# An attention layer's steps reordered on every engine, with one weight split moved to GpSimd

## What is computed

```python
def swa_sink_attention(h, w_qkv, q_gain, k_gain, sinks, w_o):
    qkv = h @ w_qkv                      # [256, 1024] @ [1024, 1536]
    ...
    q = rmsnorm(q, q_gain)               # 16 query heads of 64
    k = rmsnorm(k, k_gain)               # 4 key heads
    ...
    scores = jnp.einsum('bnqkgd,bnskd->bnkgqs', qb, kw).astype(jnp.float32) * scale
    ...
    scores = scores + alibi[None, None]
    scores = jnp.where(mask[None, :, None, None], scores, -jnp.inf)
    ...
    logits = jnp.concatenate([scores, sink_col], axis=-1)
    p = jax.nn.softmax(logits, axis=-1)[..., :-1]
    out = jnp.einsum('bnkgqs,bnskd->bnqkgd', p.astype(vw.dtype), vw)
    ...
    return out @ w_o                     # [256, 1024] @ [1024, 1024]
```

## Time and profile before

| | |
|---|---|
| Median of 3 runs | 1288.05 us (1287.56 to 1288.16) |
| Profiled execution | 1287.21 us, span 1285.4 us |
| PE busy | 1254.6 us (98%) |
| DVE busy | 894.6 us (70%) |
| ACT busy | 711.4 us (55%) |
| POOL busy | 155.2 us (12%) |
| Mean DMA rate | 175 GB/s |

### The profile page before, as it was taken

How to read it: one execution, slowest core, us unless ns; L and a number is a source line. 1 busy time by engine, 2 the same in 40 slices (tenths; PEclk the granted TensorE clock), 3 DMA queues, 4 the chain that set the end, 5 groups by cost and what they waited for, 6 DMA issues and landing times.

```text
span 1285.4 us, 19450 instructions
## 1 busy us (share of the span) xinstructions
PE 1254.6 (98%) x7940; PEld 1121.1 (87%) x7940; DVE 894.6 (70%) x1148; ACT 711.4 (55%) x909; POOL 155.2 (12%) x171
## 2 busy tenths in 40 slices
PE   8999999999799999999999999999999999999997
PEld 7889888889689888889888888889999989988886
DVE  6866656566866755568777665678899886866666
ACT  5445554455665555444764444447997873544442
POOL 0000000005604000010010000020325432100000
PEclk9999999999899999999999999999999999999999
DMA  8676665645059666666147555545544435555551
GB/s 281 201 227 178 209 196 179 200 152 191 34 147 213 204 191 196 197 164 215 66 135 255 199 185 184 187 144 161 157 153 122 153 99 193 201 196 196 196 190 41
DMA packets 214888, 224.52 MB, mean 175 GB/s; under 512 B 7312, under 2 KB 192016, under 8 KB 214672
## 3 DMA queue, kind: packets, MB, share of 16 engines
q1 hardware_dynamic: 211472, 213.41, 52.1%
q10 hardware_dynamic: 2304, 7.77, 1.8%
q0 software_dynamic: 1024, 2.10, 1.0%
HBM read 222.20 MB, written 1.05 MB: 174 GB/s over the span
## 4 chain that ended last, share of the span: by engine, by line
PE 84%; DVE 9%; ACT 3%; issue 2%; POOL 1%; DMA 1%; SPq 0%; DVEq 0%; ACTq 0%
PE ps L521 21%; PE ps L748 18%; PE ps L512 12%; PE ps L532 7%; PE ps L542 5%; PE ps L710 5%; PE ps L1040 3%; PE ps L504 3%; DVE wlo L1653 2%; PE ps L493 2%; PE ps L495 2%; PE ps L494 2%; DVE ssm_taps L2107 1%; ACT whi L1155 1%; PE ps L1021 1%
## 5 line engine op out<-in xcount | busy, mean ns | idle before, releaser
L1653 DVE TENSOR_TENSOR wlo<-raw,whi 128x2048 fp32r<-128x2048 f32 x199 | 456.5, 2300 | 127.0 <-ACT whi L1155 126.4
L1155 ACT ACTIVATE whi<-raw 128x2048 fp32r<-128x2048 f32 x202 | 385.3, 1910 | 87.9 <-PE ps L748 29.8
L521 PE MATMUL ps<-act,whi 128*128 128x512 f32 x1200 | 285.3, 390 | 0.4 <-DVE sum_sb L1796 0.4
L521 PEld LDWEIGHTS ps<-act,whi 128*128 128x128 f32 x1200 | 223.2, 188 | 45.7 <-DVE sum_sb L1796 0.7
L512 PEld LDWEIGHTS ps<-act,wlo 128*128 128x128 f32 x1416 | 180.8, 191 | 6.8 <-DVE wlo L1653 1.0
L512 PE MATMUL ps<-act,wlo 128*128 128x256 f32 x1416 | 183.9, 283 | 0.5 <-DVE wlo L1653 0.5
L1212 ACT ACTIVATE low_sb<-ps 128x512 f32<-128x512 f32 x88 | 52.4, 596 | 200.0 <-PE ps L512 199.9
L532 PE MATMUL ps<-whi,act 128*128 128x256 f32 x736 | 133.1, 285 | 1.1 <-DVE act L1734 1.1
L532 PEld LDWEIGHTS ps<-whi,act 128*128 128x128 f32 x736 | 113.5, 192 | 2.7 <-DVE act L1734 1.3
L1796 DVE TENSOR_TENSOR sum_sb<-ps,low_sb 128x512 f32<-128x512 f32 x88 | 60.5, 688 | 76.4 <-ACT low_sb L1212 76.3
L748 PE MATMUL ps<-whi,hidhi 128*128 128x512 f32 x336 | 104.2, 391 | 0.2 <-DVE sum_sb L1796 0.2
(11 more groups left out here) (238 smaller groups left out, 1848.4 us busy)
## 6 DMA issues: line engine op xcount, KB each, us to landing
raw<-in_mlp_w SPq DMA_DIRECT2D x128, 512.0 KB, 4.5
raw<-in_ffn_w_gate_up SPq DMA_DIRECT2D x88, 512.0 KB, 5.2
raw<-in_ssm_w_in SPq DMA_DIRECT2D x50, 512.0 KB, 4.8
raw<-in_ffn_w_down SPq DMA_DIRECT2D x44, 512.0 KB, 4.9
raw<-in_conv_w_in SPq DMA_DIRECT2D x24, 512.0 KB, 4.9
raw<-in_attn_w_in SPq DMA_DIRECT2D x18, 512.0 KB, 4.9
raw<-in_ssm_w_out SPq DMA_DIRECT2D x16, 512.0 KB, 4.5
raw<-in_attn_w_qkv SPq DMA_DIRECT2D x12, 512.0 KB, 4.4
```

The costliest lines, as they stand in the source:

```text
L521: e.matmul(bank2(b + f), hi[:, k, f * P:(f + 1) * P], act[:, :, k, :], start=k == 0, stop=False, skip_group_check=True)
L1155: e.activation(whi[s][:, :], raw[s][:, :], ACT.Copy).then_inc(*rounded.up(c))
L1653: e.tensor_tensor(wlo[s][:, :], raw[s][:, :], f32(whi[s][:, :]), ALU.subtract).then_inc(*split_by_vector.up(c))
```

## The change

Groups now alternate between token tiles, so that the first groups need only the first heads; the value block is projected third; attention steps are spread over blocks 3 to 5 and over the output products, on PE as below. Scores have one region (banks 2 and 3), odd groups mix in bank 5, and the output tiles gather in banks 0, 1, 7 and 2. The output weight comes in the order lower and upper columns of its first half, then of its second. On GpSimd the head rates and biases are interleaved anew, and behind the last bias it does the `lo` of block SWA + 8, which VectorE no longer does. The small per-head tiles are now six of each kind. Leaving `swa` aside, the other stages are the same.

```diff
+            return (split_by_pool if c in POOL_SPLITS.values() or c == SWA + 8 else split_by_vector)(c)
...
-            m, g = divmod(n, 4)
+            m, g = n % 2, n // 2
...
-        QKV_COLS = {"swa": (D, 0, 256, 512, 768, D + 256), "na": tuple(range(0, QKV2, WIDE))}
-        QKV_BANKS = {"swa": tuple((SWA + n) % SLOTS for n in range(5)) + (6,),
+        QKV_COLS = {"swa": (D, 0, D + 256, 256, 512, 768), "na": tuple(range(0, QKV2, WIDE))}
+        QKV_BANKS = {"swa": (1, 2, 0, 1, 0, 1),
                      "na": tuple((NA + n) % SLOTS for n in range(7)) + (6, 7)}
 
-        SCORES_AFTER = {"swa": (3, 4), "na": (5, 6)}
-
-        def score_bank(n):
-
-            return 2 * (n % 2) if n < 6 else 2
+        HEADS_OF = {"k0": 0, "k1": 0, "q0": 1, "q1": 3, "q2": 4, "q3": 5}
+        TURN_HEADS_IN = {"k0": 4, "q0": 5, "k1": 7, "q1": 7, "q2": 7, "q3": 7}
+        OUT_BANKS = {(0, 0): 0, (1, 0): 1, (0, 1): 7, (1, 1): 2}
+        SCORES_AFTER = (5, 6)
+
+        def score_bank(st, n):
+
+            return 2 if st == "swa" or n >= 6 else 2 * (n % 2)
+
+        def mix_bank(st, n):
+
+            return 6 - n % 2 if st == "swa" else 6 + n % 2
...
-                half_rows(SWA + 6 + n, A["attn_w_o"][0], n)
+                half_rows(SWA + 6 + n, A["attn_w_o"][0], 2 * (n % 2) + n // 2)
...
+                if st == "swa":
                     e.wait_ge(*qk_lo(st, f"q{g['g']}"))
-                    e.wait_ge(*qk_lo(st, f"k{g['g'] // 2}" if st == "swa" else f"k{max(g['g'] - 1, 0)}"))
-                if n == 1 and st == "na":
-                    e.wait_ge(*qk_lo("na", "q3"))
-                if n >= 2:
-                    e.wait_ge(*biased(st, n - 1 if n > 5 else n - 2))
+                    e.wait_ge(*qk_lo(st, f"k{g['g'] // 2}"))
+                    if n == 0:
+                        e.wait_ge(*copied(st, 1))
+                    else:
+                        e.wait_ge(*biased(st, n - 1))
...
+                if st == "swa" and n > 2 and n % 2:
+                    e.wait_ge(*out_lo(st, n - 2))
...
+                def heads(key):
+                    first = P * (2 * int(key[1])) + (QKV1 if key[0] == "k" else 0)
+                    e.wait_ge(*head_normed(HEADS_OF[key]))
+                    if key in ("k1", "q0"):
+                        e.wait_ge(*act_lo(2, 1, 1))
+                    elif key != "k0":
+                        e.wait_ge(*qk_lo("swa", {"q1": "k1", "q2": "q1", "q3": "q2"}[key]))
+                    turn_heads("swa", key, TURN_HEADS_IN[key], [lambda m: qkv[:, m, first:first + P],
+                                                                lambda m: qkv[:, m, first + P:first + 2 * P]])
+
+                def tokens(n, m, ks=range(KT)):
+                    if n not in opened:
+                        opened.add(n)
+                        if n > 2:
+                            e.wait_ge(*copied("swa", n - 2))
+                        e.wait_ge(*split(SWA + n))
+                    return token_products((SWA + n) % SLOTS, acthi, actlo, bank_of(QKV_BANKS["swa"][n]), m, ks, opens=m == 0)
+
+                def rows_of_out(half, col, m, pieces=(0, 1)):
+                    c = SWA + 6 + 2 * half + col
+                    e.wait_ge(*split(c))
+                    if half == 0 and 0 in pieces:
+                        e.wait_ge(*{0: copied("swa", 4), 1: copied("swa", 5), 7: qk_lo("swa", "q3"),
+                                    2: biased("swa", N_GROUPS - 1)}[OUT_BANKS[m, col]])
+                    for p in pieces:
+                        e.wait_ge(*out_lo("swa", 4 * half + 2 * p + m))
+                        last = row_products(c % SLOTS, half, OUT_BANKS[m, col], m, (2 * p, 2 * p + 1))
+                    return last
 
                 first_token_chunks(2, SWA)
...
-                for n in range(2):
-                    free[QKV_BANKS["swa"][n]] = copied("swa", n)
-                between = {3: [heads("k0", 4, 0, [head_normed(0)]), heads("q0", 6, 0, [head_normed(1)])],
-                           4: [heads("k1", 5, 2 * P, []), heads("q1", 7, 2 * P, [head_normed(2)])],
-                           5: [lambda: score("swa", 1), heads("q2", 5, 4 * P, [head_normed(3), qk_lo("swa", "k1")])]}
-                for n in range(2, 6):
-                    if n == 5:
-                        score("swa", 0)
-                    token_chunk(SWA + n, QKV_BANKS["swa"][n], between.get(n, ()))
-                    free[QKV_BANKS["swa"][n]] = copied("swa", n)
-                attend("swa", SWA + 6, 0, {0: heads("q3", 7, 6 * P, [head_normed(4), qk_lo("swa", "q1")])})
+                tokens(2, 0)
+                tokens(2, 1).then_inc(*multiplied.up(SWA + 2))
+                heads("k0")
+                tokens(3, 0)
+                heads("q0")
+                tokens(3, 1, range(0, 4))
+                tokens(3, 1, range(4, 8)).then_inc(*multiplied.up(SWA + 3))
+                heads("k1")
+                score("swa", 0)
+                tokens(4, 0)
+                score("swa", 1)
+                heads("q1")
+                tokens(4, 1, range(0, 4))
+                tokens(4, 1, range(4, 8)).then_inc(*multiplied.up(SWA + 4))
+                score("swa", 2)
+                turn_probs("swa", 0)
+                tokens(5, 0)
+                score("swa", 3)
+                turn_probs("swa", 1)
+                heads("q2")
+                mix("swa", 0)
+                tokens(5, 1, range(0, 4))
+                tokens(5, 1, range(4, 8)).then_inc(*multiplied.up(SWA + 5))
+                mix("swa", 1)
+                turn_probs("swa", 2)
+                score("swa", 4)
+                mix("swa", 2)
+                turn_probs("swa", 3)
+                rows_of_out(0, 0, 1, (0,))
+                score("swa", 5)
+                mix("swa", 3)
+                heads("q3")
+                rows_of_out(0, 0, 0)
+                score("swa", 6)
+                rows_of_out(0, 1, 0, (0,))
+                turn_probs("swa", 4)
+                score("swa", 7)
+                mix("swa", 4)
+                turn_probs("swa", 5)
+                rows_of_out(0, 1, 0, (1,))
+                rows_of_out(0, 0, 1, (1,)).then_inc(*multiplied.up(SWA + 6))
+                turn_probs("swa", 6)
+                mix("swa", 5)
+                mix("swa", 6)
+                rows_of_out(1, 0, 0, (0,))
+                turn_probs("swa", 7)
+                rows_of_out(1, 0, 0, (1,)).then_inc(*part.up("swa", 0, 0))
+                mix("swa", 7)
+                rows_of_out(1, 1, 0).then_inc(*part.up("swa", 0, 1))
+                rows_of_out(0, 1, 1).then_inc(*multiplied.up(SWA + 7))
+                rows_of_out(1, 0, 1).then_inc(*multiplied.up(SWA + 8))
+                turn_tile(3, 0, (0,))
+                turn_tile(3, 0, (1,))
+                rows_of_out(1, 1, 1, (0,))
+                rows_of_out(1, 1, 1, (1,)).then_inc(*multiplied.up(SWA + 9))
                 free.clear()
-                project("swa", SWA + 6, 3, lambda p: out_lo("swa", 4 + p), True)
+                free[0], free[1], free[2] = added("swa", 0, 0), added("swa", 1, 0), added("swa", 1, 1)
...
+            head_rate(0)
             make_bias(0)
-            head_rate(0)
+            head_rate(1)
             make_bias(1)
-            for n in range(1, 5):
-                head_rate(n)
-            for n in range(2, N_GROUPS):
-                make_bias(n)
+            head_rate(3)
+            make_bias(2)
+            make_bias(3)
+            head_rate(4)
+            make_bias(4)
+            make_bias(5)
+            head_rate(5)
+            make_bias(6)
+            make_bias(7)
+            lo(SWA + 8)
             rms_norm(3)
```

More of the change, by code:

```diff
@@ L1339, in swa @@
                 turn(0)
[L1340 to L1349 removed]
+                hi(c0 + 7)
+                exps(2)
+                turn(1)
+                mix(0)
+                heads("q2")
@@ new lines, in swa @@
+                exps(3)
+                turn(2)
+                mix(1)
+                copy(5)
+                head_square(5)
+                turn(3)
+                mix(2)
+                hi(c0 + 8)
+                exps(4)
+                mix(3)
+                heads("q3")
+                exps(5)
+                turn(4)
+                exps(6)
+                mix(4)
+                turn(5)
+                exps(7)
+                turn(6)
+                mix(5)
+                mix(6)
@@ new lines, in sum_tile @@
+                def sum_tile(m, pieces=(0, 1)):
+                    for n in pieces:
+                        if m == 0:
+                            e.wait_ge(*part("swa", 0, n))
+                        else:
+                            e.wait_ge(*multiplied(c0 + 8 + n))
+                        add("swa", ps[:, OUT_BANKS[m, n], :], m, n)
+                lo(c0 + 2)
+                head_sum(0)
+                lo(c0 + 3)
+                head_sum(1)
+                head_norm(0)
+                lo(c0 + 4)
@@ L1964, in swa @@
-                weigh(0)
```

(52 more changed lines are left out.)

173 lines of the change are left out of this document (87 added, 86 removed).

## The result

| | before | after |
|---|---|---|
| Median, runs side by side | 1287.83 us (1286.53 to 1289.13, 12 runs) | 1290.28 us (1287.24 to 1292.44, 12 runs) |
| Ratio | | 1.0017, 95% interval 1.0009 to 1.0024 |
| Profiled execution | 1287.21 us, span 1285.4 | 1290.38 us, span 1288.6 |
| PE waits, 288 to 403 us | 8.3 us | 10.0 us |

The account below looks back on a forecast made before the run. TensorE was taken as the bound, so only idle time and slow clock could be won: 11.7 - 1.0 - 2.1 - 0.5 - 2.0 - 0.95 - 1.3 = 3.85 us gain, forecast 1284.2 us, range 1280.2 to 1287.6.

Parts of the forecast that it names:

- Third block of the output weight on GpSimd: Split after the last bias: 4.6 us on GpSimd, ready 4.4 us early, cost 0, takes 2.3 us from VectorE.
- The clock: Behind the new stalls: one fall to the lower clock, a third as long as before's, costing 1.3 us.
- the second rival: Clock at the new stalls: two falls of 2.15 us each instead of one of 1.3, giving 1287.2 us; chance 0.22.
- The stalls: PE idle before the transposes of q0 (2.1 us) and q3 (2.0 us), as VectorE's splits hold GpSimd's head rates.
- The joint: Passage to the feed-forward stage: PE waits 0.95 us before the first feed-forward matmul.
- the rival "Slower": Scores on one pair of banks: PE meets the previous group's weigh unfinished, giving 1290.6 us; chance 0.07.
- the split that becomes the wait for PE: Output projection: GpSimd's split comes late and PE waits 2 us for it, giving 1286.2 us; chance 0.07.
- Middle waits: Between the two stalls: small PE waits at score 4, turn 3 and turn 5, summing to 0.5 us.
- The term for finer pieces: Layer's matmuls: more, shorter runs of the same matmuls cost PE 1.0 us of extra work.
- The 11.7 us that could be won at most: Recoverable in this layer: 8.1 us of PE idle time plus 3.6 us lost to the low clock.

Follow-up runs that it names:

- the kernel with eight pieces: Kernel after, with GpSimd's split of block SWA + 8 cut into 8 instructions of 256 columns; 1285.74 us, ratio to before 0.9985.
- the three mends: Kernel after, with block SWA + 8 split on VectorE, first bias before head_rate(0), block SWA + 7 split behind head_norm(5); 1282.55 us, again 1282.57.
- the joint's run: The three mends, with ScalarE rounding the second feed-forward block behind the first tile's activations, in this stage alone; 1280.98 us, ratio to before 0.9948.

## Why the prediction was wrong, step by step

**What failed: "Third block of the output weight on GpSimd", put at nothing.** That paragraph asked whether the block is ready when PE wants it, and it was: no PE wait of after names GpSimd's `wlo`. It also booked "It takes 2.3 us from VectorE" as relief. It did not ask what GpSimd's 4.6 us do to VectorE. The prediction told of the conflict between the two engines only in the one direction that the earlier trace rows show, a small GpSimd instruction that waits for VectorE's split; it never turned the pair round. By the same rows it could have: there a 2.28 us VectorE split stretched a 0.20 us GpSimd instruction to 2.17, and a 4.6 us GpSimd split beside VectorE's dense weigh and normalise is the same meeting with the roles exchanged. The term was 0, with room only for "one hold of 2.2" of GpSimd itself; it measured 3.0 of PE's idle time, and 2.5 of the median when undone. The trace of before even has the second direction in small: beside GpSimd's biases, which are short instructions, normalisations of 128x512 (L1918) took up to 0.94 us where 0.69 is usual.

The Trainium skill, SBUF — State Buffer, section Who interferes with whom, states the rule in both directions: VectorE with two SBUF inputs and a GpSimd instruction that reads SBUF contend, the shared ports are an exclusive lock that goes by who issues first, and a VectorE instruction with at most one SBUF input, outside the 2-port modes, is not concerned. The runs agree in the main (3.67 for 0.16 us; a one-input GpSimd instruction holds too; 0.41 and 0.18 unchanged with an input in PSUM or a single one). Less well fits the 0.86 us by which VectorE ended before the one-input instruction. The prediction had taken only the shorter sentence of the Trainium skill's GPSIMD Engine Reference, section 8 (Key points), which names the contention and no direction.

**The clock: mis-sized.** One fall "a third as long" as before's was put at 1.3; in the profiled execution there are two of that length in the layer, 3.3 together. In size that is near the second rival ("The clock falls at both stalls or for longer", 1287.2), but the falls are not at both stalls: none follows the one before q0. The first begins at 346.4, just before the q3 stall ends at 346.73; the second, at 360.0, lies 1.2 us behind the 2.95 us wait that I had not foreseen, so it may belong to the failed step. That isn't shown: in the kernel with eight pieces, whose stalls at q0 and q3 are unchanged, there was no fall in the layer, in that with the split on VectorE there were two, at other places (from 314.4 and 348.5). Each fall in the layer comes at or behind a wait of 1.6 us or more; which of these waits it follows isn't settled, and the three mends have one of 1.6 without a fall.

**The stalls: right in place and cause, near in size.** Forecast 2.1 and 2.0, released by the head norm behind a held GpSimd instruction; measured 2.8 and 2.2. GpSimd in order of time, for the first:

```profile
302.03 2.08 POOL L2412 TENSOR_SCALAR small<-small 128x8 f32<-128x8 f32 x1 [10.23 <-DVE small L2041]
...
305.95 4.62 POOL L2512 TENSOR_SCALAR bias<-table 128x128 f32<-128x128 f32 x4
310.65 0.20 POOL L2412 TENSOR_SCALAR small<-small 128x8 f32<-128x8 f32 x1
310.93 1.68 POOL L2414 TENSOR_TENSOR small<-small 128x8 f32<-128x8 f32 x1
```

The bias took 4.62 where I had 4.5, and began 0.35 late. The chain has its third instruction at 2.23 us beside VectorE's split and its first at 1.04 beside the head norm, where 0.58 is usual (2.31 for four): so the head norm does hold, by 0.5 rather than the 1.4 of its whole length. It is two instructions, of 0.70 and 0.78, so the hold is at most the first of them. The run with the first bias first removes this stall alone; the run with the norm ahead of the split removes the other.

**The rest.** The joint: 1.0 for 0.95 (the prediction's own terms, 4.65 - 3.65, give 1.0), and its cause (the rounding ahead of the activations) is shown by the joint's run. After, scores did not wait on the bias read of the group before in any sizeable way, so the rival "Slower" had the right side but the wrong mechanism; the split that becomes the wait for PE did not occur after, but did in the kernel before with the split alone (1.8 us). Middle waits: 0.8 for 0.5. The term for finer pieces, 1.0, isn't there: from 301.4 to FFN1 PE was busy 73.1 us before and 72.8 after, and less what the clock costs (3.6 and 3.3) both are 69.5.

The balance to FFN1's start, 384.07 against 378.8, is 5.2: hold 3.0, clock 3.3 - 1.3 = 2.0, stalls 0.7 + 0.2, middle 0.3, less the 1.0 of finer pieces. The 11.7 us that could be won at most did come back; the change's own waits (9.8) and falls of the clock (3.3) in the layer took 13.1, which is the 1.4 us by which FFN1 begins later. The profiled span is longer by 3.2; the other 1.8 lie behind the layer, in code that the change doesn't touch, and 1.5 of them are the fall at 1039.3. As the two profiles of the three mends show, the same kernel can have that fall in one execution and not in another, so it isn't shown to be a cost of the change.

## What to carry over

Before work is handed from VectorE to GpSimd, list VectorE's instructions with both inputs in SBUF during GpSimd's time: each can wait for the rest of the GpSimd instruction, and PE with it, even when the result of GpSimd isn't needed for long. If the work must go there, cut it into short instructions (eight of 256 columns held VectorE by about 0.5 us each, where one of 2048 held it by 3.5). And when a conflict between two engines is seen in one direction in a trace, price it in the other as well before calling a move free.

## What was unexpected of the hardware

- An instruction on 4 columns was held from 0.16 to 3.67 us, and one on 1024 columns from 1.23 to 5.53, by a GpSimd instruction of 4.6 us that had started 0.93 and 0.08 us earlier.
- A GpSimd instruction with a single SBUF input held VectorE for 3.14 us as well.
- Cutting GpSimd's work made it slower in itself (7.01 for 4.58 us) and the kernel 4.5 us faster, part of it by the clock.
- The granted clock fell to 0.50 at places that changed from kernel to kernel (none to three falls in the layer, of 3.4 to 10.2 us), and behind the layer, where the code is the same in all, in some executions and not in others (3.4 or 6.9 us, or none).
- These falls can make the spread of a kernel's runs. The 12 runs of after are spread over 5.2 us; the mean granted clock was 0.997 in the two at 1287.2 and 1287.3 and 0.993 in four of the five from 1290.96 to 1292.44 (0.994 in the other). My estimate from these numbers: a mean lower by 0.004 over 1290 us, with PE busy nearly all the time, is 5 us.
